# Routing an MoE layer tile by tile and adding gated expert rows into h in DRAM by accumulating scatters

## The chip, the cores and the metric

One core of a Trainium2 chip runs the whole program. The metric is device time in microseconds (us) of one execution; lower is better. TensorE is called PE, VectorE DVE or by its name, ScalarE ACT, GpSimd POOL, SyncE SP. SP, ACT and POOL also issue DMAs, each in its own queue and in the order of its program.

## What is computed

One decoder block: RWKV-7 time mixing and a short gated convolution side by side, merged, a product with w_o, and then an expert feed-forward with the top 4 of 32 experts. The change concerns what follows the merge:

```python
h = h + merged @ w_o                       # 1040 tokens (16 meta + 1024), 1024 channels
xf = rmsnorm(h, ln2_g)
top_v, top_i = lax.top_k(xf @ w_router + b_router, 4)
gates = softmax(top_v)
for each expert e, for the tokens that chose it:
    gt = minimum(x @ w_e_gate[e] + b_e_gate[e], 7)
    up = clip(x @ w_e_up[e] + b_e_up[e], -7, 7)
    y  = ((up + 1) * (gt * sigmoid(1.702 * gt))) @ w_e_down[e] + b_e_down[e]
    out[token] += y * gate
h = rmsnorm(h + out, lnf_g)[16:]
```

For the inputs used, the reference's router gives the 32 experts 99 to 177 tokens each: 17 experts have 99 to 128, 13 have 129 to 160, two have 162 and 177.

## The kernel before

`mixing_program` computes everything up to the merged rows mT. Its loop over j (four passes, 128 channels of the RWKV branch each) holds a serial part: for each of ten chunks the state S is multiplied by a matrix mxt on PE (L992 to L996) and VectorE makes the next state from it (L720); PE records `('s', c)` in a list of marks, and each engine waits on the marks of the others. All matmuls of this program go through the helper `mm` at L843. SP's first loads are x, the small vectors, then zeros into DRAM: `rowtok_d` and the unused end of `ys_d` (18 writes of 1 MB, L304 and L305), then the first weights.

`experts_program` begins with the w_o stage: ten tiles t of 104 tokens. PE multiplies mT by w_o into two banks (`project_out`), VectorE adds h (L1632), ACT takes squares and the root (L1503, L1505), VectorE writes the normalised rows hn (L1642), PE transposes them (L1849), ACT copies the transposes (L1496), and PE makes the router's logits (L1861). The work of tile t-1 is interleaved with the products of tile t. VectorE finds the four largest logits (`choose`, L1618). SP stores hn to DRAM as `hn_d` (L1331). SP also loads w_o and h (L356 to L361), and behind them the constants `g2_b`, `br_b` and `wr_t` (L1323 to L1325), on which the first hn waits (`const_in`).

Routing comes after the last tile, for all tiles at once (L1651 to L1734): softmax, one-hot rows, counts and ranks by two matmuls (L1868, L1871), and from these a dense list of slots. Experts are cut into rounds of 128 rows (single) or of 160 (wide: the last 1 to 32 rows beyond a full 128 ride along); `table` gives each round its expert, `starts` its first slot, `dest` each token's four slots. POOL scatters the token numbers into `rowtok_d` by 40 indirect DMAs (L1409), clears two tiles, and gathers the first round's rows (`gather`, L1425: index load L1428 and L1430, row gathers L1433 and L1438).

Then the rounds: first all wide ones, then all single ones, 34 in all (13 and 21). A round uses 12 pieces of weights of 1 MB each: 8 of gate and up, 4 of down. For each piece SP loads it into one of six buffers (L1356), ACT rounds it to w_hi (L1517), VectorE computes the rest w_lo (L1741), both into rings of four, and PE makes three products per pair (`products`, L1908 to L1910). At piece 8 of a single round PE transposes the gathered rows of the next round (`x_part`, L1886); in a wide round the four parts go before pieces 8 to 11. ACT evacuates the result at pieces 10 and 11 (y_rows L1557, overflow yo_rows L1561) and itself stores it to `ys_d` (L1589 and, four stores in a wide round, L1593). POOL's queue in round r: wait until round r's rows have landed and are transposed, gather round r+1's rows, then fetch round r+1's biases once piece 10 is begun (L1444):

```python
pool.wait_ge(rows_in[0], r * 16 + 16)
pool.wait_ge(xT_ps[3 if wide else 1], r + 1)
gather(r + 1, wide)
...
pool.wait_ge(piece_used, r * NPIECE + 10 + NRING)
get_biases(r + 1)
```

After the last round POOL gathers each token's four rows from `ys_d` (L1476, 40 gathers of 104 rows), VectorE weighs and sums them into h (L1820), ACT and VectorE apply the last norm (L1599 to L1601, L1808 to L1812), and SP writes out (L1375, L1377).

## Time and profile before

| | |
|---|---|
| three runs, median | 3109.93 us (3093.54 to 3113.36) |
| the profiled execution | 3114.73 us |
| its span in the profile | 3113.1 us |
| PE busy | 2772.0 us, 89% of the span |
| VectorE busy | 1840.0 us, 59% |
| ACT busy | 1325.3 us, 43% |
| POOL busy | 285.8 us, 9% |
| moved by DMA | 562.28 MB, 181 GB/s over the span |

The shares are averages over stages with different limits. What the change is worth is read stage by stage, from the busy time in windows, from the timelines of the single engines, and from the times that DMAs take to land. Times in the rows are us from the start of the span unless marked ns. The end of a matmul in the rows is modelled; starts are used here.

### The profile page before, as it was taken

The numbers are of one execution on the slowest core, as the hardware profiler recorded it, in microseconds if no ns is written. First come the engines' busy times: TensorE is split into PE (matmuls) and PEld (weight loads), VectorE is DVE, ScalarE is ACT, GpSimd is POOL, SyncE is SP. The second block draws the span as 40 slices with busy tenths as digits, with TensorE's granted clock in tenths as the row PEclk, the third lists the DMA queues.
The fourth block names the chain that finished last, engine by engine and source line by source line (L and its number), as shares of the span: only waits on it lengthen the run. The fifth ranks groups of instructions, "written<-read, shape, count | busy, mean of one in ns | idle before, by whom it ended". The sixth has DMA issues, their size and how long they took to land.

```text
span 3113.1 us, 55315 instructions
## 1 busy us (share of the span) xinstructions
PE 2772.0 (89%) x21189; PEld 2331.1 (75%) x21189; DVE 1840.0 (59%) x1955; ACT 1325.3 (43%) x1479; POOL 285.8 (9%) x312
## 2 busy tenths in 40 slices
PE   6998999999898999798089999999999999999960
PEld 5887877879798999544068888888788888888850
DVE  2454545464422211022457676767699999999977
ACT  2323223232211111011046565656577777777751
POOL 1010101000000000000610101010100000100023
PEclk9999988898999999899589999999999999999985
DMA  9000000000011111411247776767699999999998
GB/s 333 20 8 9 14 2 21 1 21 1 15 40 48 41 40 41 121 28 38 82 181 276 261 276 262 275 263 274 263 399 384 379 383 376 379 378 385 380 306 222
DMA packets 149040, 562.28 MB, mean 181 GB/s; under 512 B 19399, under 2 KB 73055, under 8 KB 93649
## 3 DMA queue, kind: packets, MB, share of 16 engines
q1 hardware_dynamic: 124449, 503.18, 43.6%
q0 software_dynamic: 15440, 38.14, 4.3%
q10 hardware_dynamic: 9056, 19.54, 1.6%
q8 instruction: 78, 1.28, 0.2%
q14 instruction: 17, 0.14, 0.0%
HBM read 513.10 MB, written 47.70 MB: 180 GB/s over the span
## 4 chain that ended last, share of the span: by engine, by line
PE 79%; issue 10%; DVE 4%; POOL 3%; DMA 2%; ACT 1%; SPq 0%; POOLq 0%; DVEq 0%; ACTq 0%
PE bank L843 29%; PE bank L1908 12%; PE bank L1910 12%; PE bank L1909 12%; PE bank L1917 5%; PE bank L839 2%; PE bank L919 2%; PE bank L1886 2%; POOL rowtok_d L1409 1%; POOL y_got L1476 1%; PE bank L1944 1%; PE bank L1896 1%; DMA y_got<-ys_d,dest 1%; PE bank L1923 1%; PE bank L894 1%
## 5 line engine op out<-in xcount | busy, mean ns | idle before, releaser
L1741 DVE TENSOR_TENSOR w_lo<-raw_first,w_hi 128x2048 fp32r<-128x2048 f32 x275 | 617.9, 2283 | 74.3 <-ACT w_hi L1517 74.3
L1517 ACT ACTIVATE w_hi<-raw_first 128x2048 fp32r<-128x2048 f32 x276 | 528.9, 1918 | 213.0 <-PE bank L1910 54.4
L1908 PE MATMUL bank<-w_hi,x_hi 128*128 128x512 f32 x1088 | 434.2, 399 | 2.3 <-ACT yo_rows L1561 2.3
L1910 PE MATMUL bank<-w_hi,x_lo 128*128 128x512 f32 x1088 | 425.2, 391 | 0.0
L1909 PE MATMUL bank<-w_lo,x_hi 128*128 128x512 f32 x1088 | 425.0, 391 | 0.0
L1741 DVE TENSOR_TENSOR w_lo<-raw_rest,w_hi 128x2048 fp32r<-128x2048 f32 x136 | 308.7, 2284 | 26.7 <-ACT w_hi L1517 26.7
L1517 ACT ACTIVATE w_hi<-raw_rest 128x2048 fp32r<-128x2048 f32 x136 | 258.6, 1916 | 142.7 <-DMA raw_rest<-in_w_e_down 49.6
L843 PE MATMUL bank<-xm_hi,ring_hi 128*128 128x260 f32 x896 | 261.6, 292 | 17.0 <-DVE dz L795 8.2
L843 PE MATMUL bank<-xm_hi,ring_lo 128*128 128x260 f32 x896 | 254.8, 284 | 0.0
L843 PE MATMUL bank<-xm_lo,ring_hi 128*128 128x260 f32 x896 | 254.8, 284 | 0.0
L1908 PEld LDWEIGHTS bank<-w_hi,x_hi 128*128 128x128 f32 x1088 | 204.9, 188 | 51.2 <-issue 9.0
L1910 PEld LDWEIGHTS bank<-w_hi,x_lo 128*128 128x128 f32 x1088 | 204.8, 188 | 44.2
L1909 PEld LDWEIGHTS bank<-w_lo,x_hi 128*128 128x128 f32 x1088 | 205.2, 189 | 40.8
L1908 PE MATMUL bank<-w_hi,a_hi 128*128 128x512 f32 x544 | 214.4, 394 | 0.0
L1910 PE MATMUL bank<-w_hi,a_lo 128*128 128x512 f32 x544 | 212.7, 391 | 0.0
L1909 PE MATMUL bank<-w_lo,a_hi 128*128 128x512 f32 x544 | 212.6, 391 | 0.0
L843 PE MATMUL bank<-xnT,ring 128*128 128x260 f32 x832 | 189.1, 389 | 3.9 <-DVE dz L737 3.1
L843 PEld LDWEIGHTS bank<-xm_hi,ring_hi 128*128 128x128 f32 x896 | 170.8, 191 | 19.9 <-DVE dz L795 8.4
L843 PEld LDWEIGHTS bank<-xnT,ring 128*128 128x128 f32 x832 | 160.0, 193 | 32.8 <-issue 6.2
L843 PEld LDWEIGHTS bank<-xm_lo,ring_hi 128*128 128x128 f32 x896 | 170.6, 190 | 0.9
L843 PEld LDWEIGHTS bank<-xm_hi,ring_lo 128*128 128x128 f32 x896 | 170.5, 190 | 0.0
L803 DVE TENSOR_TENSOR gt<-gt,bank 128x260 f32<-128x260 f32 x64 | 24.3, 421 | 243.6 <-ACT gt L564 243.6
(348 smaller groups left out, 4427.1 us busy)
## 6 DMA issues: line engine op xcount, KB each, us to landing
raw_first<-in_w_e_up SPq DMA_DIRECT2D x138, 1024.0 KB, 6.9
raw_first<-in_w_e_gate SPq DMA_DIRECT2D x70, 1024.0 KB, 6.7
raw_rest<-in_w_e_gate SPq DMA_DIRECT2D x70, 1024.0 KB, 6.0
raw_first<-in_w_e_down SPq DMA_DIRECT2D x68, 1024.0 KB, 8.9
raw_rest<-in_w_e_down SPq DMA_DIRECT2D x68, 1024.0 KB, 8.3
ring<-in_w_in SPq DMA_DIRECT2D x40, 512.0 KB, 4.0
ys_d<-ar SPq DMA_DIRECT2D x18, 1024.0 KB
ys_d<-y_rows ACTq DMA_DIRECT2D x34, 512.0 KB, 9.5
```

Of the source, the lines that this page charges most:

```text
L839: ins = nc.tensor.matmul(bank[b + c % 2][:, 0:CH], w[:, k, 128 * m:128 * (m + 1)], xnT[:, k, CH * c:CH * (c + 1)], start=k == 0, stop=k == ...
L843: return nc.tensor.matmul(ps, lhsT, rhs, start=start, stop=stop)
L894: ins = nc.tensor.transpose(bank[2 + q % 2][0:TP, 128 * (c - g0):128 * (c - g0 + 1)], src, ident[:, :])
L919: ins = nc.tensor.transpose(bank[6 + i % 2][0:TP, TP * m:TP * (m + 1)], Rm[:, 4 * b + m, :], ident[0:TP, 0:TP])
L1409: nc.gpsimd.indirect_dma_start(out=rowtok_d, out_offset=bass.IndirectOffsetOnAxis(ap=dest[:, a:a + 1], axis=0), in_=tok_id[:, t:t + 1], in ...
L1517: nc.scalar.activation(w_hi[:, j % NRING, :, :], raw_piece(j), ACT.Copy).then_inc(hi_done, 1)
L1741: nc.vector.tensor_tensor(w_lo[:, j % NRING, :, :], raw_piece(j), w_hi[:, j % NRING, :, :].bitcast(f32), ALU.subtract).then_inc(lo_done, 1)
L1886: ins = nc.tensor.transpose(x_bank(f, wide)[:, k * 128:(k + 1) * 128], (x_rows, xo_rows)[f // 2][:, c:c + 128], ident[:, :])
L1908: nc.tensor.matmul(ps[:, :], hi, w_hi[:, slot, k, :], start=start and k == 0, stop=False)
L1909: nc.tensor.matmul(ps[:, :], hi, w_lo[:, slot, k, :], start=False, stop=False)
L1910: ins = nc.tensor.matmul(ps[:, :], lo, w_hi[:, slot, k, :], start=False, stop=stop and k == HK - 1)
L1917: ins = nc.tensor.matmul(ps[OV * c:OV * (c + 1), 0:128], m[:, k0 + k, :], raw_piece(j)[:, k, 128 * c:128 * (c + 1)], start=start and k == ...
```

## The change

1. Routing tile by tile. `choose(u)` now also makes the gates' exponents, the one-hot rows and the running counts of tile u; a new `rank_tile` on PE makes the ranks of one tile by two small matmuls; `place(u)` gives each row a slot in a region of 1152 slots that is fixed for each expert, and the normalised gate. POOL scatters pairs (token, gate) of tile u as soon as the tile is placed. A table of rounds is made at the end from the counts alone, on 104 partitions and moved to a row by two PE transposes.
2. All slots are first filled with pad tokens (rows 1040 and up, gate 0), by three DMAs from POOL. `hn_d` and `h_d` have 128 pad rows.
3. SP also stores h to DRAM, `h_d`. ACT scales the evacuated rows by the gate. POOL adds them to `h_d` by an indirect DMA with an add, one for 128 rows and in wide rounds two more with 128 pieces of 128 channels each. The stores from ACT are gone.
4. The order of POOL's queue in a round changes with it (below), with copies of the slots (`slot_t`, `slot_ov`), since `next_t` is overwritten by the next index load.
5. The tail: SP loads h back from `h_d`, the norm is applied in place, and SP writes out. The 40 gathers and 40 weighted sums are gone.
6. The constants `g2_b`, `br_b` and `wr_t` are loaded from POOL's queue.
7. The zero writes to `rowtok_d` and `ys_d` are gone; one of 0.5 MB to the pad rows of `hn_d` takes their place.
8. Two matmuls whose result is not read follow each step of the state loop.
9. A round is wide if the expert has 129 to 160 rows (before: also, for example, 257 to 288, as one wide and one single round).

```diff
-        sp.dma_start(shared['rowtok_rows'], zero[0:shared['rowtok_rows'].shape[0], 0:shared['rowtok_rows'].shape[1]].bitcast(u32)).then_inc(zero_out, 16)
+        for rows in shared['empty_rows']:
+            sp.dma_start(rows, zero[0:rows.shape[0], 0:rows.shape[1]]).then_inc(zero_out, 16)
...
-        for rows in shared['ys_rest']:
-            sp.dma_start(rows, zero[0:rows.shape[0], 0:rows.shape[1]]).then_inc(zero_out, 16)
...
                 for h in range(2):
                     ins = mm(bank[6][hp(h), HS * (c % 2):HS * (c % 2 + 1)], mxt[hp(h), c, :], S[hp(h), c, :])
                 pe_j.mark(ins, ('s', c))
+                for h in range(2):
+                    mm(bank[2][hp(h), 0:2 * TP], mxt[hp(h), c, :], ar[hp(h), c, :, :].rearrange("p m t -> p (m t)"))
...
     def on_sync(sp):
-        sp.dma_start(g2_b, ln2_g.partition_broadcast(TP)).then_inc(const_in, 16)
-        sp.dma_start(br_b, b_router.partition_broadcast(TP)).then_inc(const_in, 16)
-        sp.dma_start(wr_t, w_router.rearrange("(k p) e -> p k e", p=128)).then_inc(const_in, 16)
...
             sp.dma_start(hn_d[TP * t:TP * (t + 1), :], hn[:, t % 2, :]).then_inc(hn_out[t % 2], 16)
+            sp.dma_start(h_d[TP * t:TP * (t + 1), :], h_all[:, t, :]).then_inc(h_out, 16)
...
-        sp.wait_ge(piece_used, rounds * NPIECE + NRING)
+        sp.dma_start(gf_b, lnf_g.partition_broadcast(TP)).then_inc(gf_in, 16)
+
+        sp.wait_ge(y_out[0], rounds * 16 + 16)
         sp.sem_inc(sp_passed, 1)
+        sp.wait_ge(y_out[1], n_wide * 32 + 32)
+        sp.sem_inc(sp_passed, 1)
+        for t in range(NT):
+            sp.dma_start(h_all[:, t, :], h_d[TP * t:TP * (t + 1), :]).then_inc(tile_got[t], 16)
         for t in range(NT):
             sp.wait_ge(fin_done, t + 1)
...
+        pool.dma_start(g2_b, ln2_g.partition_broadcast(TP)).then_inc(const_in, 16)
+        pool.dma_start(br_b, b_router.partition_broadcast(TP)).then_inc(const_in, 16)
+        pool.dma_start(wr_t, w_router.rearrange("(k p) e -> p k e", p=128)).then_inc(const_in, 16)
...
+        rows = slot_d.rearrange("(n q s) a -> n q (s a)", q=99, s=ROWS)
+        for n in range((E + 1) * SLOTS // ROWS // 99):
+            pool.dma_start(rows[n], no_slot.rearrange("q s a -> q (s a)")).then_inc(no_slot_out, 16)
+
+        pool.wait_ge(no_slot_out, 16 * ((E + 1) * SLOTS // ROWS // 99))
         for t in range(NT):
+            pool.wait_ge(dest_done, t + 1)
+            pool.wait_ge(gate_done, t + 1)
             for k in range(TOPK):
                 a = t * TOPK + k
-                nc.gpsimd.indirect_dma_start(out=rowtok_d, out_offset=bass.IndirectOffsetOnAxis(ap=dest[:, a:a + 1], axis=0),
-                                             in_=tok_id[:, t:t + 1], in_offset=None).then_inc(scattered, 16)
+                nc.gpsimd.indirect_dma_start(out=slot_d, out_offset=bass.IndirectOffsetOnAxis(ap=dest[:, a:a + 1], axis=0),
+                                             in_=tok_gate[:, a, :], in_offset=None).then_inc(scattered, 16)
...
         nc.gpsimd.memset(xo_rows, 0.0).then_inc(pads_done, 1)
         nc.gpsimd.memset(bias_t.bitcast(f32), 0.0).then_inc(pads_done, 1)
...
+        pool.dma_start(h_d[TOK:TOK + 64, :], xo_rows[OV:OV + 64, :]).then_inc(y_out[0], 16)
+        for n in range(2):
+            pool.dma_start(h_d[TOK + 64 + OV * n:TOK + 64 + OV * (n + 1), :], xo_rows[96:128, :]).then_inc(y_out[1], 16)
 
         def gather(r, wide):
 
-            start = pool.value_load(starts[0:1, bass.ds(r, 1)], min_val=0, max_val=(MAXB - 2) * ROWS)
-            pool.dma_start(idx_t[:, 0:1], rowtok_d[bass.ds(start, ROWS), :]).then_inc(idx_in[0], 16)
+            start = pool.value_load(starts[0:1, bass.ds(r, 1)], min_val=0, max_val=E * SLOTS)
+            pool.dma_start(next_t, slot_d[bass.ds(start, ROWS), :]).then_inc(idx_in[0], 16)
             if wide:
-                pool.dma_start(idx_t[0:OV, 1:2], rowtok_d[bass.ds(start + ROWS, OV), :]).then_inc(idx_in[1], 16)
+                for c in range(4):
+                    pool.dma_start(next_ov[OV * c:OV * (c + 1), :], slot_d[bass.ds(start + ROWS, OV), :]).then_inc(idx_in[1], 16)
             pool.wait_ge(idx_in[0], r * 16 + 16)
             pool.sem_inc(pool_passed, 1)
             nc.gpsimd.indirect_dma_start(out=x_rows, out_offset=None, in_=hn_d,
-                                         in_offset=bass.IndirectOffsetOnAxis(ap=idx_t[:, 0:1], axis=0)).then_inc(rows_in[0], 16)
+                                         in_offset=bass.IndirectOffsetOnAxis(ap=next_t[:, 0:1], axis=0)).then_inc(rows_in[0], 16)
             if wide:
-                pool.wait_ge(idx_in[1], r * 16 + 16)
+                pool.wait_ge(idx_in[1], r * 64 + 64)
                 pool.sem_inc(pool_passed, 1)
                 nc.gpsimd.indirect_dma_start(out=xo_rows[0:OV, :], out_offset=None, in_=hn_d,
-                                             in_offset=bass.IndirectOffsetOnAxis(ap=idx_t[0:OV, 1:2], axis=0)
+                                             in_offset=bass.IndirectOffsetOnAxis(ap=next_ov[0:OV, 0:1], axis=0)
                                              ).then_inc(rows_in[1], 16)
 
...
+        h_parts = h_d.rearrange("t (m x) -> (t m) x", x=128)
+
         gather(0, True)
         get_biases(0)
...
+        pool.wait_ge(h_out, 16 * NT)
         for first, last, wide in ((0, n_wide, True), (n_wide, rounds, False)):
             with pool.Fori(first, last) as r:
 
                 pool.wait_ge(rows_in[0], r * 16 + 16)
                 if wide:
                     pool.wait_ge(rows_in[1], r * 16 + 16)
+
+                pool.wait_ge(y_out[0], r * 16 + 16)
+                pool.wait_ge(y_out[1], r * 32 + 32 if wide else n_wide * 32 + 32)
+                pool.sem_inc(pool_passed, 1)
+                nc.gpsimd.tensor_copy(slot_t, next_t).then_inc(slot_kept, 1)
+                if wide:
+                    nc.gpsimd.tensor_copy(slot_ov, next_ov).then_inc(slot_kept, 1)
+                    nc.gpsimd.tensor_scalar(row_ov, next_ov[:, 0:1].to_broadcast([128, 2]), 8.0, None, ALU.mult).then_inc(ov_rows, 1)
+                    pool.wait_ge(ov_rows, r * 2 + 1)
+                    pool.sem_inc(pool_passed, 1)
+                    nc.gpsimd.tensor_tensor(row_ov, row_ov, part_ov, ALU.add).then_inc(ov_rows, 1)
+                    pool.wait_ge(slot_kept, r * 2 + 2)
+                    pool.wait_ge(ov_rows, r * 2 + 2)
+                else:
+                    pool.wait_ge(slot_kept, r + n_wide + 1)
+                pool.sem_inc(pool_passed, 1)
                 pool.wait_ge(xT_ps[3 if wide else 1], r + 1)
                 gather(r + 1, wide)
 
                     pool.wait_ge(piece_used, r * NPIECE + 10 + NRING)
                 pool.sem_inc(pool_passed, 1)
                 get_biases(r + 1)
-        pool.wait_ge(y_out[0], rounds * 16 + 16)
-        pool.wait_ge(y_out[1], n_wide * 64 + 64)
+                pool.wait_ge(y_read[0], r * 2 + 4)
+                pool.sem_inc(pool_passed, 1)
+                nc.gpsimd.indirect_dma_start(out=h_d, out_offset=bass.IndirectOffsetOnAxis(ap=slot_t[:, 0:1], axis=0),
+                                             in_=y_rows, in_offset=None, compute_op=ALU.add).then_inc(y_out[0], 16)
+                if wide:
+                    pool.wait_ge(y_read[1], r * 2 + 4)
+                    pool.sem_inc(pool_passed, 1)
+                    for n in range(2):
+                        nc.gpsimd.indirect_dma_start(out=h_parts, out_offset=bass.IndirectOffsetOnAxis(ap=row_ov[:, n:n + 1], axis=0),
+                                                     in_=yo_rows[:, n, :], in_offset=None, compute_op=ALU.add).then_inc(y_out[1], 16)
...
+        def gate_exp(u):
+            act.wait_ge(gexp_in, u + 1)
+            nc.scalar.activation(gates[:, u, :], gates[:, u, :], ACT.Exp).then_inc(gexp_done, 1)
...
-                        nc.scalar.activation(y_rows[:, HC * n:HC * (n + 1)], y_ps[n][:, :], ACT.Copy).then_inc(y_read[0], 1)
+                        nc.scalar.activation(y_rows[:, HC * n:HC * (n + 1)], y_ps[n][:, :], ACT.Copy,
+                                             scale=slot_t[:, 1:2].bitcast(f32)).then_inc(y_read[0], 1)
...
-                start = act.value_load(starts[0:1, bass.ds(r, 1)], min_val=0, max_val=(MAXB - 2) * ROWS)
-                act.dma_start(ys_d[bass.ds(start, ROWS), :], y_rows).then_inc(y_out[0], 16)
...
-            nc.vector.max_index(top_i[:, u, :], top_v[:, u, :], lg[:, u % 2, :]).then_inc(top_done, 1)
-
+            link(nc.vector.max_index(top_i[:, u, :], top_v[:, u, :], lg[:, u % 2, :]))
+            nc.vector.tensor_tensor(gates[:, u, :], top_v[:, u, 0:TOPK], top_v[:, u, 0:1].to_broadcast([TP, TOPK]),
+                                    ALU.subtract).then_inc(gexp_in, 1)
+            link(nc.vector.tensor_copy(top_f[:, u, :], top_i[:, u, 0:TOPK]))
+            link(nc.vector.tensor_tensor(onehot[:, u % 2, :, :], iota_e.unsqueeze(1).to_broadcast([TP, TOPK, E]),
+                                         top_f[:, u, :].unsqueeze(2).to_broadcast([TP, TOPK, E]), ALU.is_equal))
+            link(nc.vector.tensor_reduce(chosen[:, u, :], onehot[:, u % 2, :, :].rearrange("p k e -> p e k"), axis=AX.X, op=ALU.add))
+            nc.vector.tensor_tensor(before[:, u + 1, :], before[:, u, :], chosen[:, u, :], ALU.add).then_inc(chosen_done, 1)
+            dve.wait_ge(chosen_done, u + 1)
+
+        def place(u):
+
+            dve.wait_ge(rank_ps, u + 1)
+            nc.vector.tensor_tensor(rank[:, u % 2, :], bank[6 + u % 2][0:TP, E:2 * E], first_slot, ALU.add).then_inc(rank_read, 1)
+            dve.wait_ge(rank_read, u + 1)
+            link(nc.vector.tensor_tensor(slot_at[:, u % 2, :, :], onehot[:, u % 2, :, :],
+                                         rank[:, u % 2, :].unsqueeze(1).to_broadcast([TP, TOPK, E]), ALU.mult))
+            link(nc.vector.tensor_reduce(dest_f[:, u, :], slot_at[:, u % 2, :, :], axis=AX.X, op=ALU.add))
+            nc.vector.tensor_copy(dest[:, TOPK * u:TOPK * (u + 1)], dest_f[:, u, :]).then_inc(dest_done, 1)
+            dve.wait_ge(gexp_done, u + 1)
+            link(nc.vector.tensor_reduce(gsum[:, u:u + 1], gates[:, u, :], axis=AX.X, op=ALU.add))
+            link(nc.vector.reciprocal(gsum[:, u:u + 1], gsum[:, u:u + 1]))
+            nc.vector.tensor_scalar(tok_gate[:, TOPK * u:TOPK * (u + 1), 1].bitcast(f32), gates[:, u, :], gsum[:, u:u + 1], None,
+                                    ALU.mult).then_inc(gate_done, 1)
...
-            dve.wait_ge(got_in[t % NGOT], 16 * TOPK * (t // NGOT + 1))
...
-                ins = nc.vector.scalar_tensor_tensor(out=h_all[:, t, :], in0=y_got[:, t % NGOT, k, :], scalar=gates[:, t, k:k + 1],
-                                                     in1=h_all[:, t, :], op0=ALU.mult, op1=ALU.add)
...
+        def rank_tile(u):
+
+            pe.wait_ge(chosen_done, u + 1)
...
+            ps = bank[6 + u % 2][0:TP, E:2 * E]
+            nc.tensor.matmul(ps, tri, chosen[:, u, :], start=True, stop=False)
+            nc.tensor.matmul(ps, ones[:, 0:TP], before[:, u, :], start=False, stop=True).then_inc(rank_ps, 1)
+
...
+            if t >= 2:
+                rank_tile(t - 2)
...
+        rank_tile(NT - 1)
+        pe.wait_ge(wo_add, 2 * NT)
+        nc.tensor.matmul(bank[0][0:TP, 0:E], ones[:, 0:TP], before[:, NT, :], start=True, stop=True).then_inc(rank_ps, 1)
+        pe.wait_ge(q_done, 1)
+        nc.tensor.transpose(bank[2][0:1, 0:TP], q_out[:, 0:1], ident[0:TP, 0:TP])
+        nc.tensor.transpose(bank[3][0:1, 0:TP], q_out[:, 1:2], ident[0:TP, 0:TP]).then_inc(q_ps, 1)
```

## Rows read from the trace of the kernel before

**Rows 1.** Windows: us, then PE, PEld, DVE, ACT, POOL busy (count), PEclk, DMA share, GB/s

```profile
1600.00:2250.00 650.00, 640.62 (x7609) 522.01 (x7608) 454.67 (x403) 390.42 (x379) 66.12 (x63) 1.00 0.70 267
2260.00:3000.00 740.00, 740.00 (x3423) 613.23 (x3422) 705.04 (x496) 553.38 (x414) 62.36 (x60) 1.00 0.98 383
...
3070.00:3090.00 20.00, 0.00 (x0) 0.00 (x0) 16.39 (x17) 3.09 (x7) 1.26 (x2) 0.50 1.04 248
```

**Rows 2.** Timeline of VectorE and of POOL between the last tile and the rounds

```profile
1471.90 0.19 DVE L1621 TENSOR_TENSOR lg<-bank,br_b 104x32 f32<-104x32 f32 x1 [4.60 <-PE bank L1861]
...
1507.69 0.14 DVE L1734 CAST table<-total_f 1x1 uint32<-1x1 f32 x1
...
1553.55 0.99 POOL L1409 DMA_INDIRECT rowtok_d<-tok_id,dest  x1 [0.30 <-issue]
```

**Rows 3.** Timeline of the w_o stage: its first tile, and the router's matmuls

```profile
1323.54 1.28 DVE L1642 SCALAR_TENSOR_TENSOR hn<-h_all,rstd_e,g_b 104x1024 f32<-104x1024 f32 x1 [11.22 <-DMA wr_t<-in_w_router]
...
1324.88 1.65 PE L1849 MATMUL bank<-ident,hn 104*128 104x104 f32 x8 [9.41 <-DVE hn L1642]
...
1415.00 1.57 PE L1861 MATMUL bank<-wr_t,hnT 128*104 128x32 f32 x16
```

**Rows 4.** Timeline of a wide and of a single round, PE and ACT

```profile
1678.92 0.49 PE L1908 MATMUL bank<-w_hi,x_hi 128*128 128x512 f32 x1
1679.97 0.43 ACT L1561 ACTIVATE yo_rows<-bank 128x128 f32<-128x128 f32 x2
1711.58 0.66 PE L1886 MATMUL bank<-ident,x_rows 128*128 128x128 f32 x4
...
2612.19 0.39 PE L1908 MATMUL bank<-w_hi,x_hi 128*128 128x512 f32 x1
2614.22 0.58 ACT L1557 ACTIVATE y_rows<-bank 128x512 f32<-128x512 f32 x1
2635.40 1.03 PE L1886 MATMUL bank<-ident,x_rows 128*128 128x128 f32 x8
```

**Rows 5.** By tile: x_rows, y_rows (2290 to 3000), xo_rows; then waits and POOL's timeline

```profile
L1433 POOL DMA_INDIRECT x_rows<-hn_d,idx_t x20: 1078/2108/2946, 2292.2 to 2973.3; - x20
DMA to landing us min/median/max: 9.5/11.2/11.7
...
L1589 ACTq DMA_DIRECT2D ys_d<-y_rows x20: 342/346/355, 2292.2 to 2975.0; - x20
DMA to landing us min/median/max: 8.7/9.5/10.2
...
L1438 POOL DMA_INDIRECT xo_rows<-hn_d,idx_t x12: 2265/2598/2707, 1628.3 to 2198.2; - x12
...
POOL x_rows L1433 <- DMA idx_t<-rowtok_d: 78.3, 19, 5.6
...
2322.41 0.57 POOL L1428 DMA_DIRECT2D idx_t<-rowtok_d  x1 [1.10 <-issue]
```

**Rows 6.** Chain that ended last: two DMAs with no weight load beside them

```profile
1562.06 4.69 DMA x_rows<-hn_d,idx_t
...
3010.89 2.62 DMA ys_d<-y_rows
```

**Rows 7.** Windows about the stall in the w_o stage, columns as in rows 1

```profile
1319.00:1321.00 2.00, 0.00 (x0) 0.00 (x0) 0.00 (x0) 0.00 (x0) 0.00 (x0) 0.89 0.89 164
...
1329.00:1331.00 2.00, 2.00 (x4) 0.75 (x3) 0.00 (x0) 0.00 (x0) 0.00 (x0) 0.55 0.00 0
```

**Rows 8.** Windows and timeline of the state loop's end, first pass, columns as above

```profile
255.00:256.00 1.00, 0.50 (x8) 0.42 (x8) 0.28 (x1) 0.00 (x0) 0.00 (x0) 0.79 0.00 0
...
265.00:266.00 1.00, 1.00 (x18) 1.00 (x16) 0.00 (x0) 0.00 (x0) 0.00 (x0) 0.59 0.00 0
...
263.77 2.97 PE L843 MATMUL bank<-ar,S 64*64 64x104 f32 x40
```

**Rows 9.** Timeline of ACT: the last evacuation before the tail

```profile
3009.55 0.58 ACT L1557 ACTIVATE y_rows<-bank 128x512 f32<-128x512 f32 x1
```

More of the change, by code:

```diff
@@ L1110, in experts_program @@
     MAXR = shared['rounds']
-    MAXB = shared['blocks']
+    SLOTS = shared['slots']
+    MAXQ = 96
+    assert MAXR < MAXQ
     HK, HC = 4, 512
@@ L1300, in experts_program @@
     gf_in = sem("gf_in")
-    got_in = [sem(f"got_in{s}") for s in range(NGOT)]
-    sum_done = sem("sum_done")
     fsq_done = sem("fsq_done")
@@ L1645, in on_vector @@
                 choose(t - 1)
+            if t >= 2:
+                place(t - 2)
             if t == 4:
@@ L1739, in split_lo @@
+        rounds = dve.value_load(table[0:1, MAXQ:MAXQ + 1], min_val=2, max_val=MAXR - 1)
         def split_lo(n, j):
```

305 lines of the change are left out of this document (135 added, 170 removed).

## The prediction

> **What bounds the kernel now.** I read the busy time by stage first. From 1600 to 2250 us (wide expert rounds) TensorE (PE) is busy 640.6 of 650 us, from 2260 to 3000 us (single rounds) 740 of 740 at full clock; DMA is busy 0.70 and 0.98 of the time at 267 and 383 GB/s, and VectorE 705 of 740 us in the second [rows 1]. So the rounds are PE's, with little room on VectorE and DMA. Two stretches are not: the routing between the last w_o tile and the first expert product, and the tail after the last round. There I read the timeline: the last logits are read at 1471.90, the table is ready at 1507.83, the 40 scatters of token numbers occupy POOL until 1554.54 [rows 2], and the first gathered rows land at 1562.06 + 4.69 = 1566.75 [rows 6]: 94.9 us in which PE does next to nothing. The tail runs from the last evacuation (3010.13) to the end of the span, 3113.1: 103 us [rows 9]. In the w_o stage PE stands 9.4 us before the first transposes, because VectorE waits 11.2 us for the router's weights, queued on SP behind 8 MB [rows 3].
>
> The profiled execution took 3114.73 us, 1.6 beside its span, 4.8 above the median of 3109.93. I sum against it and take 5 off at the end.
>
> **Routing and w_o: -60 us.** The per-tile VectorE work (about 15 small instructions, 3.5 us) and four scatters (5.2 us, 1.3 us each: 0.99 and 0.30 of gap [rows 2]) fit in a tile of some 16 us. What is late next: tile 8 is placed only after tile 9 is chosen, so eight scatters remain. Logits at L; choose 2 us, place(8) and place(9) 3.2 us; the scatters start at L + 4 and take 10.4; beside them VectorE makes the table from some 36 instructions of 0.22 us and a PE transpose, L + 15. Landing 2 us, memsets 1.9, the added iotas and their waits 1.2, three pad writes 1.9, an index load that has become five DMAs with a wait of 2 to 4 us, then the gather: 1 us of issue and up to 9 in flight, because SP's 6 MB of weights now run beside it. Rows land at about L + 39 instead of L + 94.9: -56. The constants move from SP's queue to POOL's and no longer wait behind the 8 MB: of the 9.4 us I take back 8 (they still share the engines). rank_tile adds two matmuls a tile, each 0.2 us by the router's (1.57 us for 8) [rows 3]: +4 in all, and Exp and Sqrt now alternate on ACT, which costs only the last tile 1 us, included above. h stores (4.2 MB) lie beside 160 us of a nearly idle DMA: nothing. Sum -60; bounds -70 and -48.
>
> **Start: 0.** 18 MB of zero writes go, 0.5 MB come. PE's first work hangs on the vectors and x, which are ahead of them in SP's queue; the ring load behind them lands long before PE reaches it. Bounds -1 and +1.
>
> **Fillers in the state loop: -8.** Per head pair two state steps run with PE half idle, and the granted clock falls (0.79 of full in 255 to 256 us) and is back only in 265 to 266 [rows 8]; so some 5.4 us of matmuls after the loop run at half clock. The two added matmuls have 208 columns; twenty of 104 columns took 2.97 us [rows 8], mostly at half clock, so two of 208 take some 0.6 at half clock, 0.3 at full, about what each step idles. If the clock holds, a pass gains 3.4 us (14 in four passes); if not, it loses about 1 (4). I take -8.
>
> **Tail: -58.** The gathers, the weighted sums and their order behind the DMA go. What comes: scatter issue 1.4 and landing 6 after 3010.1, then 4.3 MB of h in and 4.3 MB out at the 248 GB/s of the old tail [rows 1], 34 us, and 4 for the last write: 45 of 103. VectorE and ACT need 1.5 us a tile, hidden. Bounds -70 and -45.
>
> **Rounds: +287, the term that decides.** Before, POOL fetches the rows of round r+1 as soon as round r's are transposed, in round r-1; the store of y hangs on ACT's queue and holds up nobody. Now POOL's queue is, in round r: wait for scatter(r-1) to land, copy the slots, gather(r+1), biases(r+1), wait for y, scatter(r). Gather(r+1) thus stands behind the landing of scatter(r-1), which can be issued only when round r-1 has ended, and PE needs the rows at piece 8 of round r. A single round takes 35.9 us (evacuation at 2614.22, the eleventh after it at 3009.55) [rows 4, 9]. In the one that begins at E = 2612.19 PE reaches those transposes at 2635.40 [rows 4]: 23.2 us are there. The chain in them:
> - the second half of y is evacuated at 2614.80: E + 2.6; semaphore 0.1;
> - accumulating scatter, issue to landing. No row shows one. Nearest: the gather of as many rows, 9.5 to 11.7, median 11.2 [rows 5], and the plain store of the same bytes, 8.7 to 10.2 [rows 5]. It reads 512 KB twice over (source and destination), so a longer flight is likely. Ends 8.7 and 20 (twice the flight of the gather); I take 13, nearest to the gather;
> - slot copy 0.4; register load before the index load 1.1 [rows 5];
> - index load 0.57 and 4.1 of waiting (78.3 us in 19 waits, 3.4 to 5.6) [rows 5];
> - gather 11.2 (9.5 to 11.7).
>
> Sum E + 33.1, so PE stands 9.9 us. Its clock then falls: in the w_o stall PE stopped at 1315.5, the clock fell within 1319 to 1321 and was back within 1329 to 1331, 6 us after work resumed at 1324.88 [rows 3, 7]; 6 us at half clock lose 3, of which I take 2.8. 12.7 us in each of the 21 single rounds: +267. Nothing hides it: the split weights are four pieces ahead and the loads six, which only gives PE its next pieces, and they keep DMA loaded throughout the chain, as in the rows. With wide rounds the rows are needed 32.7 us after the round begins (1678.92 to 1711.58) and y is complete 1.5 us in (1679.97 + 0.43) [rows 4]. Three scatters are issued one behind the other (issue of a second indirect DMA 2.6) [rows 5], the last at E + 8 and landed at E + 19.3; copies and index arithmetic 1, register 1.1, five index loads 2.7 (0.57 and four a little shorter), gather 10.2 (inside the single rounds' 9.5 to 11.7) [rows 5]: E + 34.4, a stall of 1.7 in 12 rounds, +20. ACT loses its five DMA issues in a wide round, but PE is the bound, so 0. Bounds: all low, 26.3 us in the single rounds, 3.1 us of stall and no clock, +64; all high, 18.4 + 3 in 21 rounds and 9 in 12, +557.
>
> What the Trainium skill adds: the trace has the store of y in flight for 9 us beside the weight loads, and 2.6 us alone [rows 5, 6]. "Collectives: The Full Stack", section "The bandwidth ceiling: the fold count and why AG ≠ RS ≠ AR", says that an add in the DMA engines costs not the add but two source reads on one ring, which halves the rate. No row here shows an add; by that rule the flight lies at my upper end, and the sum is rival C's.
>
> The wide rule narrows (129 to 160 rows only; before, also 257 to 288 in two rounds). The reference's router gives at most 177 rows to an expert, 13 with 129 to 160 and two with more: 13 wide and 21 single rounds under either rule.
>
> Sum: -60 + 0 - 8 - 58 + 287 = +161; 3114.7 + 161 - 5 = 3271 us.
>
> **Rivals.**
> A. The chain fits. For it: alone, gather and store take 4.7 and 2.6 us [rows 6], and with those the chain is 2.7 + 2.6 + 1.5 + 2.6 + 4.7 = 14, far inside 23.2. Against: in 20 single rounds no gather landed under 9.5. With no stall: 3110 - 126 = 2984; with all the low ends of the loaded rows 3048. It decides if scatter, index and gather together take under 19 us (I have 29).
> The Trainium skill, "DMA: Bandwidth & Descriptors", section "Anatomy of one DMA", gives 2 us plus bytes over 436 GB/s; by it each large DMA takes about 3.2 us, and rival A would come out. The trace disagrees: 9 and more beside the weight loads.
> B. The chain decides but mildly: the scatter lands like the plain store (9.5): a stall of 6.4 plus 2 in 21 rounds, +176, wide rounds nothing: 3110 + 176 - 126 = 3160.
> C. The add doubles the flight: 20 us, stall 16.9 + 3 in 21 rounds and 8 in 12: +514, 3498.
> D. The added reads make DMA the bound (0.98 busy already), without a chain: 0.5 MB more on 13.6 per round of 36 us, 1.3 us in 21 rounds, +27: 3011.
>
> **Chances.** The forecast's mechanism at its size 0.47, B 0.25, C 0.10, A 0.12, D 0.06. The measurement tells about 1% from no change. Below 3079 lie A and D, less a little for their upper ends: 0.16. Within 1%: these ends and B's lower side, 0.11. Slower: 0.73. The likeliest case's own range is 3160 to 3390 (a single round's loss of 7 to 18 us); to leave out no more than 2 in 10, C and the lower half of A, the range is 3010 to 3400.
>
> **What would show it.** PE idle before the transposes of x_rows in each single round, 8 to 12 us, with a granted clock under 1 after it; single rounds of 46 to 49 us instead of 36; wide ones 52 to 54; scatter landing 11 to 15 us; first transposes 56 us earlier relative to the last logits; tail 45 us. Wrong, if the single rounds stay at 36 us, or if they grow with PE waiting for weights instead of rows.

## Result and the profile after

The changed kernel takes 3267.97 us (median of 4 runs, 3259.15 to 3272.16) against 3107.85 us of the kernel before (here with a fourth run of it): 1.0513 times, 95% interval 1.0478 to 1.0549. It is slower by 160 us; the forecast was 3271 us.

The profiled execution has a span of 3262.6 us (before: 3113.1), so the two traces have to explain +149.5; that the medians are 160 apart and not 149.5 is the spread of single executions (the two profiled ones lie 3.8 under and 6.9 above their medians). The page gives the first hint: in the chain that ended last, DMA has 23%, and three lines of it are new.

```profile
PE 63%; DMA 23%; issue 6%; DVE 3%; ACT 2%; POOL 1%; POOLq 1%; SPq 1%; ACTq 0%; DVEq 0%
PE bank L843 28%; DMA h_d<-y_rows,slot_t 8%; PE bank L1951 6%; PE bank L1952 6%; PE bank L1953 6%; DMA x_rows<-hn_d,next_t 6%; PE bank L1864 4%; PE bank L1960 4%; DMA next_t<-slot_d 4%; DMA raw_rest<-in_w_e_down 3%; PE bank L1929 2%; PE bank L839 2%; PE bank L919 1%; POOL slot_t L1497 1%; DMA wo_t<-in_w_o 1%
...
L1929 PE MATMUL bank<-ident,x_rows 128*128 128x128 f32 x280 | 60.4, 375 | 263.0 <-DMA x_rows<-hn_d,next_t 254.8
```

Scatter 8%, gather 6%, index load 4%: these are the links of the forecast chain. The last line is the group of the transposes: PE stood idle 263 us before them, 254.8 of it until gathered rows landed.

Where the 149.5 us come from, by the same landmarks in both traces (later minus earlier, after against before):

| stretch | before | after | difference |
|---|---|---|---|
| start of the span to the end of the gate stage (DVE's last mT) | 1281.84 | 1258.02 | -23.8 |
| gate stage to the last logits read | 190.0 | 190.1 | 0 |
| last logits to first rows landed | 94.9 | 39.0 | -55.9 |
| first rows to the last evacuation of y | 1443.4 | 1732.8 | +289.4 |
| last evacuation to the end of the span | 103.0 | 42.7 | -60.3 |

**The rounds.** The windows of the single rounds, columns as in [rows 1]:

```profile
2240.00:3200.00 960.00, 743.26 (x3234) 611.32 (x3232) 672.25 (x472) 535.14 (x390) 161.69 (x99) 0.88 0.75 281
```

PE is busy 0.77 of the time, where it was busy all of it, its clock is at 0.88, and DMA fell from 0.98 [rows 1] to 0.75: no engine is the bound. One round of it on POOL (timeline: start, duration, what, and in brackets the idle time before it and what ended it):

```profile
2582.99 3.26 POOL L1520 DMA_INDIRECT h_d<-y_rows,slot_t  x1 [6.86 <-ACT y_rows L1617]
2596.18 1.55 POOL L1497 COPY slot_t<-next_t 128x2 uint32<-128x2 uint32 x1 [9.93 <-DMA h_d<-y_rows,slot_t]
2599.22 0.60 POOL L1463 DMA_DIRECT2D next_t<-slot_d  x1 [1.49 <-issue]
2605.10 1.11 POOL L1469 DMA_INDIRECT x_rows<-hn_d,next_t  x1 [5.28 <-DMA next_t<-slot_d]
2620.98 0.55 POOL L1480 DMA_DIRECT2D bias_t<-bias_d  x1 [14.77 <-issue]
2628.41 3.30 POOL L1520 DMA_INDIRECT h_d<-y_rows,slot_t  x1 [6.88 <-ACT y_rows L1617]
```

From 2582.99 on nothing overlaps on this queue: scatter 13.2, copy and register 3.0, index load 5.9, gather. PE in the same round:

```profile
2602.45 0.40 PE L1987 MATMUL bank<-bias_t,kind_row 128*128 128x512 f32 x1
2610.80 1.97 PE L1929 MATMUL bank<-ident,x_rows 128*128 128x128 f32 x8 [7.96 <-DMA x_rows<-hn_d,next_t]
```

and the windows about it (us, PE busy, granted clock, DMA share, GB/s):

```profile
2600.00:2605.00 5.00, 2.84 (x13) 1.00 1.03 426
2605.00:2610.00 5.00, 0.00 (x0) 0.68 1.01 418
2610.00:2615.00 5.00, 4.20 (x17) 0.64 0.46 190
2615.00:2620.00 5.00, 5.00 (x26) 1.00 0.00 0
```

PE stops 8 us for the rows, the clock goes to half while it stands (0.50 in the single microseconds from 2607 to 2613) and is full again from 2614 on, 3.2 us after work resumed. And a third thing is to be seen, which matters below: DMA goes from 1.01 to nothing. The weight loads have caught up with their six buffers and have stopped (SP issues a load at 2607.78 and the next only some 13 us later). This stop was a shorter one; in 19 single rounds PE waited 206.5 us for x_rows, 10.9 each, at most 12.7. The durations over the single rounds, by tile (min/median/max in ns, then us from issue to landing of the same instructions):

```profile
L1520 POOL DMA_INDIRECT h_d<-y_rows,slot_t x16: 3262/3288/3299, 2237.8 to 2973.0; - x16
...
DMA to landing us min/median/max: 12.5/13.0/13.8
```
```profile
L1469 POOL DMA_INDIRECT x_rows<-hn_d,next_t x16: 1005/2832/3079, 2260.2 to 2995.1; - x16
...
DMA to landing us min/median/max: 5.5/8.8/9.8
```

A single round takes 49.1 us (first scatter of the single rounds at 2237.81, the twentieth after it at 3220.73), 13.2 more than the 35.9 of before [rows 4, 9]. The flights answer to [rows 5]: the plain store 9.5, the gather 11.2.

**Routing and tail.** Answering to [rows 2], POOL between the logits (read at 1448.14) and the first rows: the last tiles' eight scatters, then memsets, the index loads and the gather, which lands 9.8 us later, at 1487.1.

```profile
1452.52 0.99 POOL L1437 DMA_INDIRECT slot_d<-tok_gate,dest  x1 [3.53 <-DVE tok_gate L1701]
...
1461.56 0.98 POOL L1437 DMA_INDIRECT slot_d<-tok_gate,dest  x1 [0.30 <-issue]
1464.08 0.95 POOL L1449 MEMSET xo_rows<- 128x1024 f32 x1 [1.53 <-DMA slot_d<-tok_gate,dest]
...
1468.96 0.58 POOL L1463 DMA_DIRECT2D next_t<-slot_d  x1 [0.45 <-issue]
...
1477.29 1.01 POOL L1469 DMA_INDIRECT x_rows<-hn_d,next_t  x1 [5.71 <-DMA next_t<-slot_d]
```

And SP in the tail, after the last evacuation at 3219.91 ([rows 9] before): h comes in and goes out, the two overlapping, while the span ends at 3262.6.

```profile
3227.06 4.53 SPq L1384 DMA_DIRECT2D h_all<-h_d  x10
3235.77 0.30 SPq L1388 DMA_DIRECT2D out<-h_all  x1
3237.16 15.78 SPq L1390 DMA_DIRECT2D out<-h_all  x9
```

**State loop.** The end of the loop in the first pass, in windows (us, PE busy, clock, DMA share, GB/s; [rows 8] are single microseconds of it), first before, then after; PE is given 0.69 of the clock and then all of it:

```profile
250.00:265.00 15.00, 11.15 (x161) 0.69 0.01 3
```
```profile
250.00:265.00 15.00, 13.98 (x282) 1.00 0.02 4
```

### The profile page after: what moved, and what is told of

The parts are those of the page before. It is cut to its first block, busy times and chain, and to the rows that moved or that the text cites. A ratio compares the mean times of both kernels' runs of the same rounds, so it can differ in the third digit from the quotient of the medians.

```text
span 3262.6 us, 55832 instructions
## 1 busy us (share of the span) xinstructions
PE 2807.8 (86%) x21371; PEld 2346.3 (72%) x21371; DVE 1791.3 (55%) x1997; ACT 1360.4 (42%) x1501; POOL 454.8 (14%) x463
## 4 chain that ended last, share of the span: by engine, by line
PE 63%; DMA 23%; issue 6%; DVE 3%; ACT 2%; POOL 1%; POOLq 1%; SPq 1%; ACTq 0%; DVEq 0%
PE bank L843 28%; DMA h_d<-y_rows,slot_t 8%; PE bank L1951 6%; PE bank L1952 6%; PE bank L1953 6%; DMA x_rows<-hn_d,next_t 6%; PE bank L1864 4%; PE bank L1960 4%; DMA next_t<-slot_d 4%; DMA raw_rest<-in_w_e_down 3%; PE bank L1929 2%; PE bank L839 2%; PE bank L919 1%; POOL slot_t L1497 1%; DMA wo_t<-in_w_o 1%
## 5 line engine op out<-in xcount | busy, mean ns | idle before, releaser
L1929 PE MATMUL bank<-ident,x_rows 128*128 128x128 f32 x280 | 60.4, 375 | 263.0 <-DMA x_rows<-hn_d,next_t 254.8
L1929 PEld LDWEIGHTS bank<-ident,x_rows 128*128 128x128 f32 x280 | 45.4, 193 | 277.6 <-DMA x_rows<-hn_d,next_t 238.3
L1951 PE MATMUL bank<-w_hi,a_hi 128*128 128x512 f32 x544 | 224.8, 413 | 0.0
L1952 PE MATMUL bank<-w_lo,a_hi 128*128 128x512 f32 x544 | 221.9, 408 | 0.0
L1953 PE MATMUL bank<-w_hi,a_lo 128*128 128x512 f32 x544 | 219.9, 404 | 0.0
L1794 DVE TENSOR_TENSOR a_lo<-bank,a_hi 128x512 fp32r<-128x512 f32 x68 | 46.8, 688 | 302.3 <-ACT a_hi L1586 302.3
L843 PEld LDWEIGHTS bank<-xm_hi,ring_hi 128*128 128x128 f32 x896 | 171.0, 191 | 18.9 <-DVE dz L795 8.4
```

The source lines that it names most:

```text
L843: return nc.tensor.matmul(ps, lhsT, rhs, start=start, stop=stop)
L1794: nc.vector.tensor_tensor(a_lo[part], ta_ps[:, :].rearrange("p (k s) -> p k s", k=4), a_hi[part].bitcast(f32), ALU.subtract).then_inc(alo_ ...
L1929: ins = nc.tensor.transpose(x_bank(f, wide)[:, k * 128:(k + 1) * 128], (x_rows, xo_rows)[f // 2][:, c:c + 128], ident[:, :])
L1951: nc.tensor.matmul(ps[:, :], hi, w_hi[:, slot, k, :], start=start and k == 0, stop=False)
L1952: nc.tensor.matmul(ps[:, :], hi, w_lo[:, slot, k, :], start=False, stop=False)
L1953: ins = nc.tensor.matmul(ps[:, :], lo, w_hi[:, slot, k, :], start=False, stop=stop and k == HK - 1)
```

## Experiments

The theory: a single round is lengthened by the order of POOL's queue, in which the gather of round r+1 stands behind the landing of scatter r-1. The rivals: the add itself is the cost (by its flight, or by its traffic beside the weight loads), whatever the order.

### e6: the order alone, in the kernel before

```
+                pool.wait_ge(y_out[0], r * 16 + 16)
+                pool.wait_ge(y_out[1], r * 64 + 64 if wide else n_wide * 64 + 64)
                 pool.wait_ge(xT_ps[3 if wide else 1], r + 1)
                 gather(r + 1, wide)
```

> The kernel before with one wait added: POOL fetches the rows of round r+1 only when the plain stores of round r-1 have landed; no add, no indirect write, nothing else of the change. Theory (the order alone makes the stall): evacuated at E + 2.6, store 9.2, register 1.1, index load 4.7, gather 11.2: rows at E + 28.9 where PE wants them at E + 23.2: 5.7 us of stall and 2 of clock in 21 rounds, +160: 3268 us (3190 to 3300). Rival (the indirect accumulating write is the cost, whatever the order): 3108 us as before.

Measured: 3250.46 us, 1.0442 times before (1.0395 to 1.0489). Plain contiguous stores, no indirect write, no add: and +141 us, nearly all of the +160. The store lands faster here than forecast, 8.3 us for 9.2, and the gather 9.0 for 11.2. The trace shows the same wait of PE (waits of PE over the single rounds: us in total, times, longest):

```profile
PE bank L1889 <- DMA x_rows<-hn_d,idx_t: 99.2, 21, 6.6
```

That is 4.7 us in each of the 21; 141 us are 6.7 each, and 2.0 are left, the clock's most likely (0.94 on average over the single rounds, where it was 1.00). The wide rounds took 51.8 us as before.

### e3: the changed kernel without the add

The scatters leave out the add: they overwrite the rows of h with the expert's rows, so the result is not the layer's. What is gathered and multiplied stays the same.

```
                 nc.gpsimd.indirect_dma_start(out=h_d, out_offset=..., in_=y_rows,
-                                             in_offset=None, compute_op=ALU.add)
+                                             in_offset=None)
```
(for yo_rows too)

> Leaves out the add of the scatters: they overwrite the rows of h instead; waits and order are the same. Measures what the add is worth in the landing of 12.5 to 13.8 us. If the landing is a matter of the queues of a loaded DMA and the add costs little: landing 12 to 13, 3240 to 3268 us. If it lands like the plain store of before (8.7 to 10.2): 3.7 us less of stall in 21 rounds, about 3180. If the add doubles the flight (the rival of the prediction): landing 6.5, 3110 to 3130.

Measured: 3199.2 us, 1.0277 times before (1.0253 to 1.0301), 69 us less than with the add. Between the first two expectations; the third, the doubled flight, is out. The scatter in the single rounds:

```profile
L1520 POOL DMA_INDIRECT h_d<-y_rows,slot_t x16: 2653/2668/2674, 2273.7 to 2975.5; - x16
...
DMA to landing us min/median/max: 10.7/11.1/11.5
```

So of the 13.0 us from issue to landing 1.9 are the add's; 0.6 of them lie in the issue (2.7 for 3.3). PE's wait is 8.4 us in each of 20 single rounds (168.1 in 20) where it was 10.9, and a single round takes 46.7 us, 2.4 less than the changed kernel's 49.1: nearly all of it is the shorter wait. The single rounds and the first wait of this kind, in the last wide round, give 55 us, the wide rounds and the tail 3 each: 62 between the two profiled executions, where the medians differ by 69. The remaining +91 us over the kernel before are there without any add.

### e1: the gather ahead of the wait

The slots of the next round are copied to a tile of their own (held_t), and the gather goes ahead of the wait for the scatter; the scatter's own copy is taken from held_t.

```
-                pool.wait_ge(y_out[0], r * 16 + 16)
-                ...
-                nc.gpsimd.tensor_copy(slot_t, next_t).then_inc(slot_kept, 1)
+                nc.gpsimd.tensor_copy(held_t, next_t).then_inc(slot_held, 1)
+                ...
                 gather(r + 1, wide)
+                pool.wait_ge(y_out[0], r * 16 + 16)
+                ...
+                nc.gpsimd.tensor_copy(slot_t, held_t).then_inc(slot_kept, 1)
```

> Edit: the slots of the next round are copied to a second pair of tiles, so that POOL issues the index load and gather of round r+1 ahead of its wait for the landing of scatter r-1; the scatters and their adds are the same. Theory (the chain through the landing sets the stall): scatter issued at E + 2.6 for 3.3 us, copy and register 1.5, index load 5.6, gather 2.9 of issue and 5.9 to landing: rows at about E + 22 where PE wants them at E + 23.2. Single rounds fall from 49.1 us to 36 to 38, 20 or 21 times: 3268 - 230 to 275 = 2993 to 3038 us. Rival (the add's own traffic slows the loads, and the wait is only where it shows): single rounds stay above 44 us, 3160 us or more.

Measured: 3110.11 us, 1.0004 times before (0.9987 to 1.002). 158 us of the loss go with the wait, with the add and all its bytes still there, so of that part the wait was the cause and not the traffic. But the expectation was missed by some 70 us: single rounds take 41.2 us and not 36 to 38. POOL's timeline says why:

```profile
2566.93 3.29 POOL L1529 DMA_INDIRECT h_d<-y_rows,slot_t  x1 [6.83 <-ACT y_rows L1626]
2569.61 2.59 POOL L1497 COPY held_t<-next_t 128x2 uint32<-128x2 uint32 x1
2573.74 0.60 POOL L1466 DMA_DIRECT2D next_t<-slot_d  x1 [1.53 <-issue]
2581.01 1.49 POOL L1472 DMA_INDIRECT x_rows<-hn_d,next_t  x1 [6.68 <-DMA next_t<-slot_d]
```

The scatter is no longer waited for, but it is still in flight, and POOL now waits 7.1 us for the small index load beside it (128.1 in 18; I had 5.6), and the copy behind the issue 2.6 where I had 0.4. The gather is issued 14.1 us after the scatter and lands 8.7 later: with the scatter's issue at E + 3.5 (here E = 2563.42, the round's first matmul, as in the prediction) that is E + 26.3, 3.1 us too late. PE waited 66.6 us in 19 rounds, 3.5 each. The queue's order was a chain even without its longest link.

### e2: the gather two rounds ahead

As e1, but the rows of round r+2 are fetched in round r once the rows of r+1 are transposed; a third tile of slots (next, held, current) makes room.

```
+                nc.gpsimd.tensor_copy(held_t, next_t).then_inc(slot_held, 1)
+                ...
+                pool.wait_ge(xT_ps[3 if wide else 1], r + 2)
+                gather(r + 2, wide)
                 pool.wait_ge(y_read[0], r * 2 + 4)
                 nc.gpsimd.indirect_dma_start(out=h_d, ..., compute_op=ALU.add)
```

> Edit: as the first one, with the gather still earlier: rows of round r+2 are fetched in round r, as soon as the rows of r+1 are transposed, so that no landing of that round stands ahead of them. Theory (chain): no wait of PE for x_rows in the single rounds at all, 36 us each: 3268 - 21 x 13.1 = 2993 us, and if the loads had wanted the bytes anyway (0.5 MB more beside 13.6 MB a round at a DMA share of 0.97) 37.3 us each, 3020. Against the first edit: the same or up to 20 us faster. Rival (the add's traffic): 3160 or more.

Measured: 2990.62 us (2986.76 to 2993.05), 0.9612 times before (0.9594 to 0.9631): 119 us faster than before and 277 faster than the change. No PE instruction waits for x_rows in a single round any more. Window (columns as in [rows 1]) and POOL's timeline:

```profile
2260.00:2900.00 640.00, 640.00 (x2960) 530.32 (x2959) 610.16 (x429) 483.88 (x357) 145.74 (x106) 1.00 1.00 380
```
```profile
2588.00 1.04 POOL L1472 DMA_INDIRECT x_rows<-hn_d,next_t  x1 [4.36 <-DMA next_t<-slot_d]
2589.34 1.62 POOL L1537 DMA_INDIRECT h_d<-y_rows,slot_t  x1 [0.30 <-issue]
2602.29 1.61 POOL L1504 COPY slot_t<-held_t 128x2 uint32<-128x2 uint32 x1 [11.32 <-DMA h_d<-y_rows,slot_t]
```

The scatter still takes 13 us, and now nobody needs it sooner. PE is busy throughout at full clock; a single round takes 35.9 us (scatter at 2553.40, the next at 2589.34), exactly as before the change. DMA is at 1.00 and yet not the bound: the added reads cost nothing that can be seen, so the prediction's rival D is out as well. The two steps of the order together, e1 and e2, make up the whole of the single rounds' 13.2 us.

### e8: one link more

The index load is made twice, one behind the other (the second copy into a tile that is not read).

```
+            pool.dma_start(again_t, slot_d[bass.ds(start, ROWS), :]).then_inc(again_in, 16)
+            if not wide:
+                pool.wait_ge(again_in, r * 16 + 32)
             nc.gpsimd.indirect_dma_start(out=x_rows, ..., in_=hn_d, ...)
```

> The changed kernel with the index load made a second time, into a tile that nobody reads, between the first one and the gather; in the single rounds POOL also waits for it. Theory (the chain has no slack left in a single round): issue 0.6 and landing 5.6 more, 6 us in 21 rounds, and up to 1 us more of clock in each: 3268 + 126 to 147 = 3394 to 3415 us. Rival (part of the chain lies beside something else that PE waits for, such as weights): less than 60 us more, under 3330.

Measured: 3302.5 us, 1.0633 times before (1.0602 to 1.0664): 35 us more than the change and not 126 to 147. By the numbers the rival, and yet PE waits for rows and not for weights. What happened stands in the landing of the gather (tile x_rows, single rounds):

```profile
L1479 POOL DMA_INDIRECT x_rows<-hn_d,next_t x20: 1007/1007/1024, 2259.7 to 3227.6; - x20
...
DMA to landing us min/median/max: 4.1/4.3/5.2
```

and in the windows of one stop (us, PE busy, clock, DMA share, GB/s):

```profile
2610.00:2615.00 5.00, 0.00 (x0) 0.84 0.99 395
2615.00:2620.00 5.00, 0.00 (x0) 0.50 0.82 279
2620.00:2625.00 5.00, 2.97 (x11) 0.50 0.08 33
```

The second index load took 5.6 us from its issue to the gather's, but the gather then flew 4.3 us instead of 8.8: by then PE had stood so long that the weight loads had filled their buffers and stopped, and the gather met less of them. That takes 4.5 of the 5.6 us back; PE waits 12.3 us a round (245.8 in 20) for 10.9, and a single round takes 50.9 us for 49.1. The chain has no slack, but its links are not constants: they are as long as the loads beside them make them, and a stop long enough ends the loads.

### e4 and e5: the filler matmuls

```
                 for h in range(2):
-                    mm(bank[2][hp(h), 0:2 * TP], mxt[hp(h), c, :], ar[hp(h), c, :, :].rearrange("p m t -> p (m t)"))
```
taken out of the changed kernel (e4), and the same lines put into the kernel before (e5).

> The changed kernel without the two filler matmuls per head pair and state step; the outputs are those of the reference. The traces say that the state loop is 26 us shorter with them (they held the granted clock at 1.00 where it fell to 0.69 in 250 to 265 us before): 3268 + 26 = 3294 us. The prediction's term says 8: 3276. If the 26 us come from elsewhere in the change: 3268.

> The kernel before with the two filler matmuls alone. By the traces' difference 3108 - 26 = 3082 us; by the prediction's term 3100; if they only take time, 3112.

Measured: e4 3295.12 us (1.0585 times before, 1.0555 to 1.0615), 27 more than the change; e5 3083.31 us (0.9914, 0.9891 to 0.9937), 26 less than before. The two agree: the fillers are worth 26 us, wherever they stand, and not 8. The clock goes with them, in e4 and then in e5 (columns as under "State loop"):

```profile
250.00:265.00 15.00, 11.15 (x173) 0.72 0.01 2
```
```profile
250.00:265.00 15.00, 13.99 (x263) 1.00 0.01 3
```

### e7: constants later

On e2, POOL's loads of constants and its slot writes wait for the first half of w_o.

```
         pool.wait_ge(gate_mul, 3 * KT * 4 + 6)
+        pool.wait_ge(wo_in[0], 16)
         pool.dma_start(g2_b, ...)
```

> The kernel that fetches rows two rounds ahead (2990.6 us), with POOL's loads of constants and its slot writes held until the first half of w_o has landed. In the changed kernel PE waits 13.3 us for that half and 3.7 us for the second, with 0.9 MB of constants and slots beside them; before, 11.5 and 0.4. Theory (these shared bytes gave back half of the 9.4 us stall that was removed): the two waits fall by 1.5 to 4 us together, and 2987 to 2989 us. Rival (the first half is late for another reason, or the constants now come late for the first tile): no change, or 2 to 8 us slower, with a wait of VectorE for the router's weights.

Measured: 2985.84 us (2978.96 to 2993.39), 0.9614 times before (0.959 to 0.9639), for e2 0.9612: no difference, the theory's 2 to 4 us being too small for the spread of these runs. The traces decide. PE's timeline, e2 and then e7 (the gate stage ends at 1256.9 and at 1251.9):

```profile
1268.32 10.10 PE L1882 MATMUL bank<-wo_t,mT 128*104 128x512 f32 x16 [13.43 <-DMA wo_t<-in_w_o]
1280.63 15.68 PE L1882 MATMUL bank<-wo_t,mT 128*104 128x512 f32 x32 [2.22 <-DMA wo_t<-in_w_o]
1296.15 0.88 PE L1911 MATMUL bank<-ident,hn 104*128 104x104 f32 x8
```
```profile
1260.75 9.88 PE L1882 MATMUL bank<-wo_t,mT 128*104 128x512 f32 x16 [10.80 <-DMA wo_t<-in_w_o]
1275.27 16.33 PE L1882 MATMUL bank<-wo_t,mT 128*104 128x512 f32 x32 [4.63 <-DMA wo_t<-in_w_o]
1291.44 0.88 PE L1911 MATMUL bank<-ident,hn 104*128 104x104 f32 x8
```

The first wait fell by 2.6 us and the second rose by 2.4. The first transposes come 39.3 and 39.5 us after the gate stage. The theory had the two waits fall by 1.5 to 4 us together, and they fell by 0.2: it is refuted.

## Why the prediction was right, and where it was not

- **Rounds, +287: measured +289.** By the evacuations of y it is +264 in the 20 periods from one single round to the next, +12 in the one from the last wide round to the first single one, and +12 in the 12 from one wide round to the next. The mechanism is shown from three sides: the wait alone, without add, costs 141 us (e6); without the wait 158 us go (e1); without the chain the single rounds are back at 35.9 us (e2). The single round's +12.7 came as +13.2: 10.9 of stall (forecast 9.9), and 2.3 are left, mostly the clock's (forecast 2.8): in four stops, read in single microseconds, it stays at half for 3.2 to 4.7 us after work resumes. Inside the chain errors cancel. The scatter is issued at E + 3.5 (E = 2579.47 in the round shown above, and 3.5 in the other rounds too) where I had 2.7, and landed after 13.0, as taken. Copy and register took 3.0 for 1.5 (the copy alone 1.5 for 0.4), the index load 0.6 and 5.6 of waiting (89.6 in 16) for 0.6 and 4.1, and the gather 8.8 for 11.2: together about E + 34.7 where I had 33.1. That the gather came 2.4 us early is luck for the sum. Why it did isn't shown. Where I wrote that the loads "keep DMA loaded throughout the chain, as in the rows", the windows show DMA going to nothing at the end of a stop, and e8 shows what that can be worth; but in e1 the gather issued at 2581.01 lands after 8.7 us too, and there the DMA share is 1.01 in both windows from 2580 to 2590. A dry stream can't be the whole reason.
- **Wide rounds, +1.7 each: measured about +1.0, for another reason.** The period (from the evacuation of round 0 to that of round 12, over 12) is 52.8 us for 51.8. The step that failed is the chain for wide rounds: PE does not wait for rows at all. The scatters of yo_rows, the last of a wide round, landed 6.8 us after their issue (at the median) where I had 11.3, and the gather of x_rows 7.1 after its own where I had 10.2. What PE waits for instead is VectorE's x_lo and a_lo (6.6 us in 7 waits and 2.2 in 4, none of either before), behind late weights. The chain of waits has a load of raw_rest of 9.3 us at this place (issued 1784.14, landing 1794.0), while POOL's two gathers fly (issued 1777.81 and 1784.73); before, the load of the same piece, with no gather beside it, landed in 4.9 (1807.46 to 1812.32). ACT splits pieces in order, so its x_hi and VectorE's x_lo come late and PE stops about a microsecond. In e2, where the gathers lie elsewhere, another piece (raw_first of w_e_down) stands in the chain and the period is 52.9; without the add (e3) it is 52.6. So most of it is there without the add; which transfer it is was not separated.
- **Rival B** (the scatter lands like the plain store) is out: the flight was 13.0 against 9.5. It was the nearest miss: e6, where a plain store stands in that place, lost 6.7 us a round where B had 8.4. **Rival C** is refuted in this case. "Collectives: The Full Stack", section "The bandwidth ceiling: the fold count and why AG ≠ RS ≠ AR", in the Trainium skill has, for reduce-scatter collectives, an add cost a second source read and half the rate; here the scatter with the add flew 13.0 us and without it 11.1. **Rival A** needed the three DMAs under 19 us; they took 28.0 (13.0, 0.6 and 5.6, 8.8). The Trainium skill's 2 us plus bytes over 436 GB/s ("DMA: Bandwidth & Descriptors", "Anatomy of one DMA") would give, as an estimate, about 3.2 us for each large one; the measured landings beside the loads are 8.8 and 13.0. In e8, with less of the loads beside it, the gather comes to 4.3, about what it took alone (4.69) [rows 6]. **Rival D** is refuted by e2.
- **Routing, -56: measured -55.9.** Logits + 39.0, as worked out; inside it the wait for the index load was longer (5.7 us for 2 to 4).
- **Tail, -58: measured -60.3.** 42.7 us and not 45.
- **w_o stage, -8 and +4: measured -4 and +4.** From the gate stage to the first transposes 39.0 us instead of 43.0, and from there to the last logits 151.1 instead of 147.0 (a tile takes 16.26 instead of 15.92, and the last one has its own delay). The step that failed is "of the 9.4 us I take back 8". The stall for the router's weights is gone, but the constants, with the slot writes 0.9 MB, now come beside the 8 MB of w_o and the rows of x: the waits for w_o grew from 11.5 and 0.4 us to 13.3 and 3.7. The other traces bear the growth out (together 15.7 to 17.0 us in e1 to e4 and e8, 11.3 and 12.8 in e5 and e6, which have the loads of before), but not the exact gain: in e5 the stall for the router's weights is 6.5 us and the first transposes come after 39.7. PE's timeline, before ([rows 3] have what follows) and after:

```profile
1291.37 9.71 PE L1834 MATMUL bank<-wo_t,mT 128*104 128x512 f32 x16 [11.54 <-DMA wo_t<-in_w_o]
1301.49 13.98 PE L1834 MATMUL bank<-wo_t,mT 128*104 128x512 f32 x32 [0.42 <-DMA wo_t<-in_w_o]
```
```profile
1269.33 8.48 PE L1864 MATMUL bank<-wo_t,mT 128*104 128x512 f32 x16 [13.34 <-DMA wo_t<-in_w_o]
1281.50 15.68 PE L1864 MATMUL bank<-wo_t,mT 128*104 128x512 f32 x32 [3.69 <-DMA wo_t<-in_w_o]
1297.02 0.88 PE L1893 MATMUL bank<-ident,hn 104*128 104x104 f32 x8
```

  e7 shows that moving them again only moves the wait. From 1262 to 1277 us the changed kernel's DMA share is 1.01 to 1.05, which fits a stretch where every byte wanted before the first transposes counts, whichever queue brings it; no run leaves the bytes out, so that is argued and not shown.
- **Start, 0: measured +2.7 between the two traces, which says little.** The first product of the LoRA matrices starts at 49.4 instead of 46.7; the chain has the load of conv_w at 16.4 us, 13.4 before. But the traces of the experiments, whose start is that of one of these two kernels, have it at 44.6 (e4), 45.0 (e8) and up to 50.3 (e3) with the change, and at 48.5 (e5) and 49.8 (e6) without. The term of 0 is neither borne out nor refuted; what was wrong is to bound it at -1 and +1 from one trace.
- **State loop, -8: measured -26** (e5, e4), outside my bounds of -14 and +4. I asked for the 5.4 us after each loop that ran at half clock. The windows before show the clock low for longer: 0.89 in 235 to 250, 0.69 in 250 to 265, 0.97 in 265 to 280, and in the second pass, 415 to 460, 0.87, 0.67 and 0.77. From 205 to 945 us the clock averaged 0.92 before and 0.97 after. The step that failed is "so some 5.4 us of matmuls after the loop run at half clock": the mechanism was right (e5: clock 0.96 in that stretch and 26 us less), its size was not. I had read one pass of four (two windows of 1 us), and the second pass lost more.

The sum stands at +149.4 against the forecast's +161: rounds +2, routing 0, tail -2, w_o +4, start +3, state loop -18. That 3271 and 3268 lie 3 us apart is luck on top of a right mechanism: the terms miss by 11.5 us in sum, and by 18 in one of them, and the spread of executions gave most of it back (the median of the changed kernel is 3.8 above its profiled execution, that of before 6.9 under its own). Two slips of the sums changed nothing: with an index wait of 5.6 us the "all high" stall is 18.9 and not 18.4 us (+567 for +557), and the wide rounds' chain counts the issue of five index loads without a wait for the first to land.

## What to carry to other kernels

When a queue gets a wait for a completion (here: the landing of an accumulating write), add up everything queued behind it, and ask when the first consumer needs its result; the cure here was not a cheaper write (e3: 3199 us) but another order and one more buffer of slots of a kilobyte, with its like for the wide rounds (e2: 3268 to 2991 us). Here a small DMA was as long as what flew beside it made it (the index load's wait 5.6 us, 7.1 in e1), so removing one link of such a chain can lengthen the others (e1) and adding one can shorten them (e8). To size a clock effect read all passes in windows, not the one that shows it best.
